# Keys of sample 0 scored one page per half tile over thirteen steps, and page numbers read by GpSimd ahead of its wait

## What is computed

```python
k_past = cache_k[i][page_table].reshape(dec_b, n_past, HC, DC)   # 16 pages of 512 KB a sample
z = einsum('bqhd,bshd->bhqs', q, k) * d ** -0.5 + offset         # scores
log_rest = where(mask, log_sigmoid(-z), 0.0)
between = cumsum(log_rest, reverse=True) - log_rest
out = einsum('bhqs,bshd->bqhd', exp(log_sigmoid(z) + between), v)
```

## Time and profile before

| | us |
|---|---|
| median of 3 runs | 2438.76 |
| the runs | 2429.02, 2438.76, 2443.66 |
| the profiled execution | 2441.72 |
| span of its records | 2440.2 |
| TensorE busy | 2238.2 (92%) |
| VectorE busy | 1161.6 (48%) |
| ScalarE busy | 598.4 (25%) |
| GpSimd busy | 192.3 (8%) |

### The profile page before, as it was taken

One profiled execution on the slowest core, in us unless ns is written; L12 is line 12 of the kernel. 1 busy time (PEld: TensorE's weight loads), 2 busy tenths in 40 slices (PEclk: granted clock), 3 DMA queues, 4 the chain that ended last, 5 costly groups with the idle time before them and its releaser, 6 DMA issues.

```text
span 2440.2 us, 45909 instructions
## 1 busy us (share of the span) xinstructions
PE 2238.2 (92%) x17191; PEld 1977.7 (81%) x17191; DVE 1161.6 (48%) x3560; ACT 598.4 (25%) x741; POOL 192.3 (8%) x301
## 2 busy tenths in 40 slices
PE   6799999999998989689979987999999998999997
PEld 2189888888887978689968887888788787788997
DVE  1542333424243343434363256776677766755332
ACT  1322121212122121222232232232222222233221
POOL 0000101101010101000000001011011011000110
PEclk9899899989999899879989999999999999999999
DMA  9977454545645464223442245777878877854442
GB/s 317 315 218 214 141 173 155 150 147 160 192 148 164 133 182 155 71 73 110 119 143 75 73 122 200 261 254 257 268 244 270 274 239 240 267 181 130 135 130 61
DMA packets 400019, 437.02 MB, mean 179 GB/s; under 512 B 16916, under 2 KB 306990, under 8 KB 399167
## 3 DMA queue, kind: packets, MB, share of 16 engines
q1 hardware_dynamic: 359270, 311.99, 41.9%
q0 software_dynamic: 30752, 113.67, 13.4%
q10 hardware_dynamic: 9810, 8.73, 1.1%
HBM read 407.79 MB, written 26.54 MB: 178 GB/s over the span
## 4 chain that ended last, share of the span: by engine, by line
PE 66%; DVE 15%; DMA 8%; issue 5%; ACT 4%; POOLq 1%; POOL 0%; DVEq 0%; SPq 0%; ACTq 0%
PE pt L507 50%; PE m L507 14%; DMA arena<-in_cache_k 6%; DVE arena L1636 4%; ACT arena L916 2%; ACT w_hi L916 2%; DVE w_lo L1276 1%; DMA raw<-in_e_w_ada 1%; PE m L511 1%; DMA arena<-in_o_k_norm_g 1%; POOLq L1878 1%; DVE arena L1447 1%; PE pt L511 0%; DVE arena L1794 0%; DVE arena L1393 0%
## 5 line engine op out<-in xcount | busy, mean ns | idle before, releaser
L507 PE MATMUL pt<-act_hi,w_hi 128*128 128x260 f32 x4384 | 924.1, 293 | 63.6 <-DVE act_lo L1359 23.2
L507 PE MATMUL pt<-act_hi,w_lo 128*128 128x260 f32 x4384 | 897.0, 287 | 0.0
L507 PE MATMUL pt<-act_lo,w_hi 128*128 128x260 f32 x4384 | 896.7, 287 | 0.0
L507 PEld LDWEIGHTS pt<-act_hi,w_hi 128*128 128x128 f32 x4384 | 693.1, 194 | 126.5 <-issue 96.8
L1276 DVE TENSOR_TENSOR w_lo<-raw,w_hi 128x1024 fp32r<-128x1024 f32 x274 | 335.3, 1224 | 906.7 <-ACT w_hi L916 906.2
L507 PEld LDWEIGHTS pt<-act_lo,w_hi 128*128 128x128 f32 x4384 | 693.2, 193 | 0.0
L507 PEld LDWEIGHTS pt<-act_hi,w_lo 128*128 128x128 f32 x4384 | 691.0, 193 | 0.0
L916 ACT ACTIVATE w_hi<-raw 128x1024 fp32r<-128x1024 f32 x274 | 289.6, 1057 | 1170.3 <-PE pt L507 1155.0
L1636 DVE CUSTOM_DVE_ANT_0 arena<-arena 128x128 f32<-128x128 f32 x1024 | 224.9, 286 | 104.8 <-DMA arena<-in_cache_k 104.5
L916 ACT ACTIVATE arena<-arena 128x1040 f32<-128x1040 f32 (+8 forms) x199 | 169.7, 864 | 281.2 <-DVE arena L1730 81.7
L507 PE MATMUL m<-arena 128*128 128x128 f32 (+7 forms) x1136 | 210.0, 348 | 6.9 <-POOL arena L1939 4.1
(11 more groups left out here) (161 smaller groups left out, 1096.6 us busy)
## 6 DMA issues: line engine op xcount, KB each, us to landing
arena<-in_cache_k POOLq DMA_DIRECT2D x128, 512.0 KB, 4.9
arena<-in_cache_v SPq DMA_DIRECT2D x128, 512.0 KB, 5.1
raw<-in_o_w_in SPq DMA_DIRECT2D x112, 512.0 KB, 5.6
raw<-in_e_w_in SPq DMA_DIRECT2D x98, 512.0 KB, 4.4
raw<-in_e_w_ada SPq DMA_DIRECT2D x96, 512.0 KB, 5.7
raw<-in_o_w_ada SPq DMA_DIRECT2D x96, 512.0 KB, 5.4
raw<-in_e_w_out SPq DMA_DIRECT2D x32, 512.0 KB, 4.1
raw<-in_o_w_out SPq DMA_DIRECT2D x32, 512.0 KB, 4.8
```

Source lines behind the costliest of these rows:

```text
L507: return pe.matmul(out, lhsT, rhs, start=start, stop=stop, skip_group_check=True)
```

## The change

`key_pages`, which scored two pages, now calls `key_page` twice, which scores one. In l1b the order stays what it was. In l1a `KEYS0_AT` now has an entry for every page: pages 0 to 9 have a step each (23 to 32), and steps 33, 34 and 35 have two each. Before, the first page was scored in step 26 and the last two in step 34. On POOL `value_load` stands ahead of the wait for `k_free` instead of behind it, in l1a and in every pass of l1b.

```diff
--- before.py
+++ after.py
@@ -65,7 +65,7 @@
 
 Q_AT, V_AT = [4, 8, 13, 17], [22, 26, 31, 35]
 L1A_STEPS = 36
-KEYS0_AT = [26, 27, 28, 29, 30, 32, 33, 34]
+KEYS0_AT = [23, 24, 25, 26, 27, 28, 29, 30, 31, 32, 33, 33, 34, 34, 35, 35]
 KEYS_AT = [1, 3, 4, 5, 7, 8, 9, 10]
 
 
@@ -1624,18 +1624,22 @@
                 step(stt(y, y, GELU, x, ALU.mult, ALU.mult))
                 return ts_(y, y, -40.0, None, ALU.max)
 
+            def key_page(b, p, to):
+
+                if p == 0:
+                    dve.wait_ge(s("qb"), b * 16 + 16)
+                slot = key_slot(p)
+                dve.wait_ge(s(f"page{slot}"), b * 128 + 16 * (p // 2 + 1))
+                for h in range(HC):
+                    kpage = pages[:, slot, P * h:P * h + P]
+                    last = dve.tensor_tensor_reduce(kpage, kpage, qb[:, P * h:P * h + P], 1.0, 0.0,
+                                                    ALU.mult, ALU.add, to[:, 8 * p + h:8 * p + h + 1])
+                last.then_inc(s("k_free"), 1)
+
             def key_pages(b, k, to):
 
-                if k == 0:
-                    dve.wait_ge(s("qb"), b * 16 + 16)
-                for p in range(2):
-                    dve.wait_ge(s(f"page{p}"), b * 128 + 16 * (k + 1))
-                    for h in range(HC):
-                        kpage = pages[:, p, P * h:P * h + P]
-                        at = 8 * (2 * k + p) + h
-                        last = dve.tensor_tensor_reduce(kpage, kpage, qb[:, P * h:P * h + P], 1.0, 0.0,
-                                                        ALU.mult, ALU.add, to[:, at:at + 1])
-                    last.then_inc(s("k_free"), 1)
+                for p in (2 * k, 2 * k + 1):
+                    key_page(b, p, to)
 
             def pair(r):
                 return g23 if r % 2 else g01
@@ -1669,8 +1673,9 @@
                         value_gate(r, n - V_AT[r])
                     if n == Q_AT[3] + 2:
                         copy(qcol.rearrange("p (b h) -> p h b", b=NB), wide[:, 0:HC, T:N]).then_inc(s("q_col"), 1)
-                    if n in KEYS0_AT:
-                        key_pages(0, KEYS0_AT.index(n), zs[0])
+                    for p in range(NPAGE):
+                        if n == KEYS0_AT[p]:
+                            key_page(0, p, zs[0])
                     yield
 
             mix = l1a_mix()
@@ -1872,10 +1877,10 @@
 
             def key_page(b, p):
                 first = isinstance(b, int) and b == 0
+                page = pool.value_load(ptab[0:1, bass.ds(b * NPAGE + p, 1)], min_val=0, max_val=NPOOL - 1)
                 if p >= 2 or not first:
                     pool.wait_ge(s("k_free"), b * 16 + (p - 1))
                     pool.sem_inc(s("pool_waited"), 1)
-                page = pool.value_load(ptab[0:1, bass.ds(b * NPAGE + p, 1)], min_val=0, max_val=NPOOL - 1)
                 pool.dma_start(pages[:, key_slot(p), :], ck[bass.ds(page, 1)].rearrange("n s d -> (n s) d"))\
                     .then_inc(s(f"page{key_slot(p)}"), 16)
```

## The result

The changed kernel takes 2407.94 us, the median of 4 runs (2401.09 to 2411.82), against 2438.65 (2429.02 to 2443.66): a ratio of 0.985 (95% interval 0.981 to 0.989), so it is faster by 30.7 us. The forecast was 18.5. The profiled execution took 2404.32 us where the one of before took 2441.72, which is 37.4 us less. All ratios here leave out executions that took over 1.5% more than the fastest one of their kernel; that matters in one place, the 19 of before beside the first group of experiments, where five go (four of 2454 to 2460 us and one of 3136.73 us) and the other 14 have a median of 2441.9 us.

What follows compares the result with a forecast made beforehand. The prediction took TensorE, with 66% of the chain, as the bound. Gains of 13 us in l1a and 5.5 us in l1b, 18.5 in sum, took the median from 2438.8 to 2420.3 us; range 2408 to 2431.

Steps and rivals of the forecast that it cites:

- l1a: Stage before l1b: spreading sample 0's key pages over more steps gains 13 us, bounds 11 and 15.
- walked: Hand-stepped timing of VectorE, ScalarE, TensorE and POOL through l1a's steps 23 to 35, trusted to a microsecond.
- The stall: In l1a, TensorE's longest wait for `w_lo`, near 1451 us, falls from 8.0 to 3.6 us.
- the last wait: At the end of l1a, TensorE's wait for the scores grows from 4.7 to about 8 us.
- The release: On POOL, each slot release reaches the key load's issue 0.55 us sooner, some 0.7 us after sem_inc.
- Five passes x 1.1 = 5.5 us, bounds 0 and 8.3: In l1b, two releases per pass, for pages 5 and 7, each come 0.55 us sooner in five passes.
- The forecast of the evidence: In the profile after, l1b's TensorE waits for L1684 come near 18 us in all, not 24.
- A: l1b's key loads land no sooner on shared DMA engines, read ahead gives 0: 2425.8 us; 0.17 together with E.
- B: In l1b the clock comes back too: read ahead gives 8.3 us plus 6 from matmuls, 2411.5 us; chance 0.11.
- C: In l1a the gate and page pairs eat the gain, leaving 7 us: 2426.3 us; chance 0.08.
- E: On POOL, a read issued ahead makes the wait seen late, giving 0: time of A; 0.17 together with A.
- D: In l1b, key loads get in front of value loads, value pages come late, 31 us lost: 2451 us; chance 0.04.

Runs made afterwards that it cites:

- the first group of experiments: Three kernels on one chip against before: new order with read behind, old order with read ahead, new order with two reads behind; ratios 0.9953, 0.9884, 1.0078.
- The order alone: New order of the keys of sample 0, page number still read behind the wait, against before: 2431.67 us, ratio 0.9953.
- the second pair: Second profiles of the unchanged and the changed kernel on a third chip: l1b 701.7 and 687.0 us, medians 2443.53 and 2405.36 us.
- the read alone: Old order of the keys of sample 0, page number read ahead of the wait, against before: 2412.32 us, ratio 0.9884.
- e9_values_later: New order, read behind the wait, SP reading the page number three more times ahead of value pages 5 and 7, against before: 2413.22 us, ratio 0.9887.
- the second group of experiments: Later altered kernels, measured against before; the text doesn't list which kernels belong to this group.
- e3_read_twice: New order with the page number read twice behind the wait, against before: 2458.36 us, ratio 1.0078.

## Why the prediction was wrong, step by step

**l1a, right.** L1734 begins in this row, 1502.9 if the 7.1 us by which the launch reached the first gate later are taken off (forecast 1504.1; before in the earlier trace rows):

```profile
1509.99 0.29 DVE L1734 SCALAR_TENSOR_TENSOR arena<-arena,per_head 128x128 f32<-128x128 f32 x1
```

The matmuls behind it come at 1517.99, so 1510.9 (forecast 1510.7 to 1512.1). Less the same 7.1 us, pages 0 to 2 begin at 1424.7, 1428.2 and 1433.6 as walked, page 3 at 1442.3 and page 4 at 1447.8 (walked 1442.2 and 1447.7), and `w_lo` behind it at 1449.5 (1449.4). The stall is 3.79 us (3.6); no page up to 10 is awaited; the last wait is 8.23 us (some 8). The order alone was to give 11.5 us: 0.47% of 2445.1 is 11.5. TensorE waits 5.9 us for `w_lo` in all (some 6). Only the late pages were a little off: page 11 waits 1.05 us and not 3.7, page 12 waits 2.59, page 13 0.69 and not 2.8.

**The release, right.** From POOL's sem_inc to the issue it is 0.69 us (forecast 0.7; the earlier trace rows has 1.24), in the chain of after:

```profile
1491.65 0.02 POOLq L1883
...
1491.73 0.04 POOLq L1884
...
1491.80 0.03 POOLq L1884
...
1492.34 6.81 DMA arena<-in_cache_k
```

**l1b, the term of the sum that was mis-sized.** "Five passes x 1.1 = 5.5 us, bounds 0 and 8.3" failed: the first pair of profiles gives 30.5 us, the second pair 14.7, the read alone some 21 to 25 in the medians. In the first pair 20.9 us of it are shorter waits, and 10.0 are matmuls at a higher clock, a term that the sum put at nothing because waits of 2.8 us were expected to stay. The step took the landing of pages 5 and 7, 7.55 and 7.00 us, as fixed and shifted it by the 0.55 us of the release. But a landing time is no property of the load. It goes with the place of the issue among those of SP (5.2 us in the median 1.5 us or more ahead of the value pair, 7.4 with it or behind), and here a shift of about 1 us was enough to change that. The trace of before could have said so: in its good pass 3 the loads of pages 5 and 7, issued 1.33 and 1.08 us ahead of SP's pair, landed in 5.3 and 4.5 us and not in 7.55 and 7.00 as in the bad pass 1. I used their difference to say that there is nothing to gain in the good ones, and didn't ask what makes a pass good.

The forecast of the evidence failed in the same place: TensorE's waits for L1684 were to fall to some 18 us and fell to 3.1.

**The rivals.** A named the right resource with the wrong sign: it said that shared engines would make an earlier issue worthless, and in these runs it was worth about four times its 5.5 us. The page "DMA: Bandwidth & Descriptors" of the Trainium skill (Issuing engines are not separate DMA queues) says that DMAs of all issuers interleave on the same 16 engines. The runs agree that they are shared (with short value loads the key loads land in 4.3 us in the median, against 4.9), and add that the place of the issue, by a microsecond or two, moves the landing of page 5 by some 2 us. B had the direction (2411.5, the nearest to 2407.94) and one of its two causes: with the waits gone the granted clock stays at 1.00, and the same 20 matmuls take 4.60 us in place of 6.29. Its bound of 8.3 us for the landing was the same mistake. C (7 us of l1a, measured 13.9) and E (nothing from the read, measured 21 to 25) fell. D didn't come true for this change (no wait for value pages stands out in after), but `e9_values_later` shows that value pages have little slack: held back by three reads, they cost 5.0 us in three waits.

**The range.** It ended at 2408 because B was given 4 us of its own and no more. 2411.5 less 4 is 2407.5, so rounding alone put 2407.94 outside; an end a little lower would have held the result by luck, with the step above just as wrong. The scatter of the three runs of before, 14.6 us, and the passes of two kinds in its trace were a reason for a wider end on the fast side. The 16 runs of before beside the second group of experiments spread over 28.6 us (2431.05 to 2459.68).

## What to carry to other kernels

Where a wait ends with a DMA that shares its engines with another issuer, as the key loads here do, don't carry its landing time over unchanged: list the issues of both queues for a good and a bad repetition of the same loop, and see which comes first. A change of half a microsecond can then be worth what separates the two kinds of repetition, not half a microsecond. And if the urgent load can't be issued sooner, the one beside it may be issued later: three idle reads on SP gave back 16 us.

## What the runs showed of the hardware

- Reading a page number into a register behind a wait costs POOL 0.55 us per load, of which the load itself is 0.29 us. Ahead of the wait it costs nothing that shows; two of them behind it cost twice (1.09 us from the first TENSOR_LOAD to the row that computes the address, in pass 1 of `e3_read_twice`).
- A 512 KB load of keys lands in 3.6 us at least, 4.9 to 5.0 in the median and up to 7.3 to 8.1 us in the launches of after and before; where the value loads beside it are short, 4.3 us in the median and at most 6.7.
- One program differs from execution to execution by which of its passes are long; against after's 676.8 us the profiles have 3 to 8 us more of l1b for each long pass (13 in `e9_values_later`, which also waits for values). On one chip 12 runs of before spread over 19 us and 17 others over 34 us.
- The stage up to the first gate, with the same instructions, ends within 1411.2 to 1427.6 us in different executions. What makes this difference was not looked into.
